# Transformer layer in fp32 pairs: the passage between the output projection and FFN2, and two orderings in the late FFN1 groups

## The reference

```
m_lat = silu(c) @ ada_w + ada_b          # nine shift/scale/gate vectors, also for c_ctx
x   = x   + 0.5 * m_lat[2] * swiglu(modulate(rms_norm(x, g1),   m_lat[0], m_lat[1]), W1in, W1out)
ctx = ctx + 0.5 * m_ctx[2] * swiglu(modulate(rms_norm(ctx, g1), m_ctx[0], m_ctx[1]), W1in, W1out)
mix = concat(retention(hx, hc), latent_attention(hx, hc)) @ mix_w_out
x   = x + m_lat[5] * mix
x   = x + 0.5 * m_lat[8] * swiglu(modulate(rms_norm(x, g3), m_lat[6], m_lat[7]), W2in, W2out)
out = rms_norm(x, final_g)
```

## Time and profile before

| | |
|---|---|
| profiled execution, its own time | 2855.02 us |
| its span | 2853.2 us |
| median of three runs | 2856.29 us |
| PE busy | 2775.5 us (97%), 12983 matmul records |
| PE weight load busy | 2293.5 us (80%) |
| DVE busy | 1699.8 us (60%) |
| ACT busy | 901.1 us (32%) |
| mean granted PE clock | 0.993 |
| chain that ended last | PE 83%, DVE 4%, ACT 3%, issue 2%, DMA 2% |

### The profile page before, as it was taken

The page is one execution under the profiler, slowest core; times in us unless marked ns, Lnnn a source line. Parts: engine busy times, 40 slices in busy tenths (PEclk is TensorE's granted clock), DMA queues, the critical chain, the costliest instruction groups (busy, mean ns, idle before and its releaser), DMA issues.

```text
span 2853.2 us, 33123 instructions
## 1 busy us (share of the span) xinstructions
PE 2775.5 (97%) x12983; PEld 2293.5 (80%) x12983; DVE 1699.8 (60%) x1740; ACT 901.1 (32%) x830; POOL 7.0 (0%) x15
## 2 busy tenths in 40 slices
PE   6999999999999999999999899999989999999998
PEld 4778888888888888878877788887878888888886
DVE  6866756666575756565645843465564555555556
ACT  6631212122121212112112522354353333333333
POOL 0000000000000000000000000000000000000000
PEclk9999999999999999999999999999999999999999
DMA  9956555555554657676755442432355555555553
GB/s 312 303 193 191 170 150 158 163 160 162 147 176 132 196 158 255 191 245 188 232 170 176 111 118 89 131 106 80 118 171 173 187 186 190 191 191 190 182 188 132
DMA packets 408016, 496.83 MB, mean 174 GB/s; under 512 B 19090, under 2 KB 277512, under 8 KB 407176
## 3 DMA queue, kind: packets, MB, share of 16 engines
q1 hardware_dynamic: 407196, 493.10, 55.3%
q0 software_dynamic: 496, 2.63, 0.3%
q10 hardware_dynamic: 252, 0.10, 0.0%
HBM read 493.69 MB, written 2.10 MB: 174 GB/s over the span
## 4 chain that ended last, share of the span: by engine, by line
PE 83%; DVE 4%; ACT 3%; issue 2%; DMA 2%; SPq 0%; DVEq 0%; ACTq 0%
PE py L944 8%; PE py L946 8%; PE py L945 8%; PE pg L944 5%; PE pg L946 5%; PE pg L945 5%; PE pu L946 5%; PE pu L945 5%; PE pu L944 5%; ACT wh L562 2%; PE py L1378 2%; PE py L1380 2%; PE py L1379 2%; PE pg L1359 1%; PE pg L1360 1%
## 5 line engine op out<-in xcount | busy, mean ns | idle before, releaser
L1450 DVE TENSOR_TENSOR wl<-raw,wh 128x2048 fp32r<-128x2048 f32 x342 | 783.7, 2291 | 832.5 <-ACT wh L562 832.3
L562 ACT ACTIVATE wh<-raw 128x2048 fp32r<-128x2048 f32 x342 | 654.1, 1914 | 1361.8 <-PE py L946 495.8
L944 PE MATMUL py<-ah,wh 128*128 128x512 f32 x704 | 276.8, 393 | 6.2 <-DVE xy L1612 5.1
L946 PE MATMUL py<-ah,wl 128*128 128x512 f32 x704 | 274.8, 390 | 0.0
L945 PE MATMUL py<-al,wh 128*128 128x512 f32 x704 | 274.6, 390 | 0.0
L944 PE MATMUL pu<-hh,wh 128*128 128x512 f32 x656 | 255.8, 390 | 0.0
L944 PE MATMUL pg<-hh,wh 128*128 128x512 f32 x656 | 255.5, 389 | 0.0
L946 PE MATMUL pu<-hh,wl 128*128 128x512 f32 x656 | 255.2, 389 | 0.0
L946 PE MATMUL pg<-hh,wl 128*128 128x512 f32 x656 | 255.2, 389 | 0.0
L945 PE MATMUL pu<-hl,wh 128*128 128x512 f32 x656 | 255.2, 389 | 0.0
L945 PE MATMUL pg<-hl,wh 128*128 128x512 f32 x656 | 255.2, 389 | 0.0
(11 more groups left out here) (420 smaller groups left out, 4605.2 us busy)
## 6 DMA issues: line engine op xcount, KB each, us to landing
raw<-in_ffn_w_in SPq DMA_DIRECT2D x170, 1024.0 KB
chunk<-in_ada_w SPq DMA_DIRECT2D x189, 512.0 KB, 3.9
raw<-in_ffn_w_out SPq DMA_DIRECT2D x88, 1024.0 KB
raw<-in_ada_w SPq DMA_DIRECT2D x64, 512.0 KB
raw<-in_mix_w_in SPq DMA_DIRECT2D x30, 1024.0 KB
accc<-in_ada_w SPq DMA_DIRECT2D x35, 512.0 KB, 4.7
raw<-in_mix_w_out SPq DMA_DIRECT2D x16, 1024.0 KB
war<-in_ffn_w_in SPq DMA_DIRECT2D x16, 384.0 KB, 5.1
```

Source lines behind the costliest of these rows:

```text
L562: nc.scalar.activation(wh[:, slot % 2, :], raw[:, slot, :], ACT.Copy).then_inc(wh_ready, 1)
L944: mm(out_ap, w[0], xh_ap, start=first, stop=False, skip_group_check=True)
L946: return mm(out_ap, w[1], xh_ap, start=False, stop=last, skip_group_check=True)
L1450: tt(wl[:, slot % 2, :], raw[:, slot, :], wh[:, slot % 2, :].bitcast(F32), ALU.subtract).then_inc(wl_ready, 1)
```

## The change

Three parts, and no arithmetic is changed.

**Passage.** The natural turns get a new order (`NATURAL`): the four of the gate first, then the eight of x. Turns 0 to 2 stand ahead of `square_sums(1)`, turns 3 to 5 behind it, and the remaining six behind half slabs 3, 4 and 5. `diag` moves to another place in memory (where low tiles 8 to 15 will be written) and DVE makes it ahead of the last output slabs. ACT loads the root's table ahead of the last squares, copies turns 0 and 1 ahead of the root, turns 2 to 5 behind tile 3, and the rest behind the tiles. DVE forms the low half of FFN2's second slab behind tile 3 in place of ahead of tile 0.

**Late loop.** In steps 8 and later no chunk piece goes ahead of the evictions.

**Last group.** SP issues the two input pieces ahead of the two chunk loads.

```diff
-    diag = at("diag", [P, KT, P], F32, o_e)
+    diag = at("diag", [P, KT, P], F32, o_hl + 8 * KB)
+    NATURAL = (8, 9, 10, 11, 0, 1, 2, 3, 4, 5, 6, 7)
 SP:
             for s in range(GSLABS - RAW):
                 ahead(LASTG, s)
+                x_piece(2 * s)
+                x_piece(2 * s + 1)
                 for t in (2 * s, 2 * s + 1):
                     chunk_load(8 * D + CH, t, t % 2, CHUNK0 + 3 * SINGLE_CHUNKS + t)
-                x_piece(2 * s)
-                x_piece(2 * s + 1)
 ACT:
             for s in range(8):
                 if s < 7:
                     static_split(MIX0 + S_OUTM + s + 2)
+                else:
+                    link(nc.scalar.activation(dummy[:], dummy[:], ACT.Sqrt))
                 for t in (2 * s, 2 * s + 1):
                     square(1, t, Y_OUT + HEADS + s + 1)
+            natural(0)
+            natural(1)
             roots(1)
             static_split(FFN2_0 + 1)
             for t in range(KT):
                 hh_tile(1, 0, ml[:, 6 * KT:7 * KT], t)
+                if t == 3:
+                    for p in range(2, 6):
+                        natural(p)
             for j in range(3, 8):
-                natural(2 * j - 6)
-                natural(2 * j - 5)
+                if j < 6:
+                    natural(2 * j)
+                    natural(2 * j + 1)
 PE:
+            natural_turn(0)
+            natural_turn(1)
+            natural_turn(2)
             square_sums(1)
+            for p in range(3, 6):
+                natural_turn(p)
             for j in range(8):
                 half_slab(0, FFN2_0 + j, ...)
-                if j >= 2:
-                    natural_turn(2 * j - 4)
-                    natural_turn(2 * j - 3)
+                if 2 < j < 6:
+                    natural_turn(2 * j)
+                    natural_turn(2 * j + 1)
 DVE:
-                    if units == 2 and todo:
+                    if units == 2 and todo and s < 2 * GROUP:
                         chunk_ops(*todo[0])
                         todo = todo[1:]
             static_split(MIX0 + S_OUTM + 1)
+            for t in range(KT):
+                ins = ts(diag[:, t, :], eyes[:, 0, :], g3l[:, t:t + 1], None, ALU.mult)
+            ins.then_inc(diag_ready, 1)
             roots(1, 0)
-            static_split(FFN2_0 + 1)
             for t in range(KT):
                 hl_tile(1, 0, xl, a3l, ml[:, 6 * KT:7 * KT], t)
+                if t == 3:
+                    static_split(FFN2_0 + 1)
+                    ve.wait_ge(nat_turned, 4)
-            for t in range(KT):
-                ins = ts(diag[:, t, :], eyes[:, 0, :], g3l[:, t:t + 1], None, ALU.mult)
-            ins.then_inc(diag_ready, 1)
```

More of the change, by code:

```diff
@@ L859, in _, with natural @@
             static_split(MIX0 + S_OUTM + 1)
+            def natural(p):
+                j = NATURAL[p]
+                se.wait_ge(nat_turned, p + 1)
+                dst = xn[:, j // 4, (j % 4) * 512:(j % 4 + 1) * 512] if j < 8 else g3b[:, (j - 8) * 512:(j - 7) * 512]
+                nc.scalar.activation(dst, py[p % 4][:], ACT.Copy).then_inc(y_free, 1)
             for s in range(8):
@@ L873, in _ @@
             link(nc.scalar.activation(dummy[:], dummy[:], ACT.Silu))
[L875 to L878, removed]
             def silu(i, m):
@@ L905, in _ @@
                 static_split(FFN2_0 + j + 2)
-            natural(10)
-            natural(11)
             with se.Fori(0, GROUPS - 2) as i:
@@ L1347, in _, with natural_turn @@
                     out_slab(MIX0 + S_OUTM + s, py[s], HEADS)
+            def natural_turn(p):
+                j = NATURAL[p]
+                pe.wait_ge(y_free, Y_F2 + p - 3)
+                if p == 0:
+                    pe.wait_ge(diag_ready, 1)
+                for t in range(4):
+                    o = py[p % 4][:, t * P:(t + 1) * P]
+                    if j < 8:
+                        ins = nc.tensor.transpose(o, xl[:, 4 * (j % 4) + t, (j // 4) * P:(j // 4 + 1) * P], ident)
+                    else:
+                        ins = mm(o, ones[:], diag[:, 4 * (j - 8) + t, :], start=True, stop=True)
+                ins.then_inc(nat_turned, 1)
+            natural_turn(0)
+            natural_turn(1)
+            natural_turn(2)
             square_sums(1)
+            for p in range(3, 6):
+                natural_turn(p)
             def half_slab(i, m, banks, quarter, first_tile=None):
@@ L1384, in down_slab @@
                         ins.then_inc(y_done, 1)
[L1386 to L1396, removed]
             pe.wait_ge(y_free, Y_F2)
```

## The result

| | before | after |
|---|---|---|
| median of the runs | 2855.81 us (4 runs, 2853.49 to 2858.62) | 2834.97 us (4 runs, 2833.67 to 2836.46) |
| profiled execution | 2855.02 us | 2833.67 us |
| its span | 2853.2 us | 2831.9 us |
| mean granted PE clock | 0.993 | 0.994 |

The ratio is 0.9924, with a 95% interval of 0.9912 to 0.9936: faster by 20.8 us. Between the two profiled executions it is 21.35 us.

A forecast was written before the change was run, and what follows sets the result against it. PE was taken as the bound (83% of the last-ending chain), with waits at three places: 6.7 + 8.8 + 5.7 = 21.2 us off 2855.02 gives 2833.8, plus 1.27 to the runs' median: 2835.1 us, range 2830 to 2842.

The forecast's parts named there:

- Last group, 8.8: Last group: PE's waits for x and ctx over seven slabs vanish once input pieces go first; 8.8 us gained.
- The ring rival: Last group: late chunk loads close SP's queue on itself, 18 us a slab, about 2879 us in all; chance 0.03.
- The 6.6 us of slack: Last group: chunk loads are used 6.6 us after the last lands; the ring forms only if they land later than that.
- Passage, 2.14 + 3.56 = 5.7: Passage: half slab 4 starts 2.14 us earlier, two gate pairs leaving PE's later stretch save 3.56; loop 5.7 us earlier.
- The wait ahead of half slab 3: Passage: DVE and ACT set the pace up to tile 15, so PE waits some 1.4 us there.
- the tiles' start: Passage: with the split gone from their front, DVE's tiles begin 2.1 us earlier.
- The rival "bound further on": Passage: slabs 5 to 7 also wait for ACT and DVE, only 2.14 us is left, 2838.7 us; chance 0.12.
- what the prediction left at 0 to 0.5: Passage: cost if the clock stays low behind the gap and the first half slab ends a microsecond later; 0 to 0.5.
- Late loop, 5.9 + 1.7 - 0.9 = 6.7: Late loop: eviction stalls gone 5.9 us, low clock behind one stall 1.7, less 0.9 new lateness at step 10; 6.7 gained.
- Its 0.3 a group: Late loop: the fourth load's piece comes 0.1 to 0.2 us late for step 10's turns, with the semaphore 0.3 a group.
- One of the prediction's signs of being wrong: Anywhere in the kernel: low clock in new places, listed among the observations that would show the prediction wrong; no size given.
- The rival that the prediction drew from it: Late loop: each stall could cost 0 or 1.7 us in another execution, returning 0 to 5.1, not 1.7; no chance given.

The follow-up runs named there:

- e5: The kernel before with one step alone: DVE forms the low half of FFN2's second slab behind tile 3, not ahead of tile 0; 2852.55 us.
- e4: The changed kernel with one step taken back: DVE forms the low half of FFN2's second slab ahead of tile 0 again; 2837.72 us.
- e3: The kernel before with only the passage's edits, late loop and last group as before; 2849.84 us.
- e2: The kernel before with only the input pieces issued ahead of the chunk loads in the last group; 2847.34 us.
- e7: The changed kernel with the first chunk piece of step 8 put between the evictions and the split; 2834.50 us.
- e1: The kernel before with only the late loop's edit, no chunk piece ahead of the evictions in step 8; 2849.97 us.
- e9: The changed kernel again, unedited, timed beside other kernels; 2835.71 us.
- f2: The changed kernel again, unedited, timed in another set on another chip; 2834.22 us.
- e6: The changed kernel with the passage's later splits behind tiles 6, 9, 12, ACT's copies behind the splits and Silu's table load later; 2835.22 us.

## Why the prediction was right

The time (2835.1 forecast, 2834.97 measured) came out by its own steps in two places. In the third the steps were right and the size belonged to one execution, so that the closeness of the total is in part luck.

**Last group, 8.8.** Measured 8.70, and 8.68 alone. The argument was one of order: the pieces' load is issued when its buffer is free and not behind two loads that wait for DVE. It also lands sooner than I took (median 3.6, not 4.8). The two chunk loads no longer stand just ahead of it; that this is the reason isn't shown. The ring rival asked that chunk loads land late; in the trace they are issued 3.6 us later than the pieces and hold nobody. The 6.6 us of slack in it was read too large: in before's trace the second of the two loads lands at 1464.85 and its operation starts at 1470.43, 5.6 us later. In the changed kernel these are 1457.36 and 1463.75, 6.4 us.

**Passage, 2.14 + 3.56 = 5.7.** Measured 2.36 + 3.53 = 5.89. e5 and e4 give each term by itself (2.44 and 3.60). The wait ahead of half slab 3 was 1.15 where I had 1.4. The square sums came 0.1 late, as worked out (2077.32 - 2074.53 = 2.79 against 2.68). The missing 0.2 is the tiles' start: 2.3 us earlier and not 2.1. What the prediction doesn't say is that some 1.1 of this term (the estimate above) is time that the low clock had cost the kernel before. The rival "bound further on" fell: no wait ahead of half slabs 5 to 7. e3 answers what the prediction left at 0 to 0.5, a low clock in the changed kernel: 0.

**Late loop, 5.9 + 1.7 - 0.9 = 6.7.** Measured 6.3 between the two profiled executions, in the mean 4.8. The table's rows take it apart. Late loop less stalls is 362.01 - 5.09 = 356.92 in before and 361.02 - 4.09 = 356.93 in e2; both had a stretch of low clock. It is 358.21 - 2.91 = 355.30 in e3 and 358.61 - 3.30 = 355.31 in e5, which had none. So one such event costs 1.62 (I had 1.7). With neither stall nor wait it is 354.41 (three executions), so a stall costs 0.89 / 3 = 0.30 beside its idle time (I had 0.26; e7's order differs too, so this is an estimate). Beyond these 354.41 the changed loop takes 0.3 to 1.3, mean 0.8, which I put down to the new wait (I had 0.9). Its 0.3 a group doesn't follow from its own numbers: 1141.2 + 3.9 + 1.28 is 1146.38, 0.03 and not 0.1 to 0.2 behind 1146.35. The load took 4.0 (1140.86 to 1144.86), and PE waited 0.29. On average each price came out within 0.1 us. What was mis-sized is the count: idle 5.1 where four executions have 5.1, 4.1, 2.9 and 3.3, and one clock event where four have two. The mean is 3.85 + 0.9 + 0.8 - 0.8 = 4.8. The prediction said this of the clock and not of the stalls. Their length hangs on when a 512 KB load lands: in all twelve DVE's first piece waited for its load, and PE's idle time is that wait less 0.22 (2.11 and 1.89 in the earlier trace rows).

Why did the time still come out? By the traces' means the change is worth 19.4, and 21.2 was forecast. Before's profiled late loop was 2.0 over its mean, but that execution was short elsewhere: 0.4 below the mean of thirteen executions up to group 7's first turns (1091.04 against 1091.44), 0.6 below it from slab 8 to the projection's end (545.64 against 546.27). So its total was an ordinary one (0.8 below the median of the runs shown above), which takes up about half of the 2.0. The rest is luck as far as the runs show: the medians say 20.4 to 20.8 and the three stretches 19.4, and those 1.0 to 1.4 us are not explained.

One of the prediction's signs of being wrong did show, low clock in a new place: the changed kernel's profile has 6.8 us of it from 50.2 us on, where before's has none. It lies ahead of all that was changed, and e1, e4, e9 and f2 have it there too (3.4 to 6.8 us) and the other seven not, e2 and e3 among them.

The Trainium skill ("TensorE: Matmul & The Clock Gate", "What's actually happening") has the clock judged in a rhythm that is independent of the kernel. The runs are in line with that: of twelve eviction stalls two were followed by low clock, group 8's 2.25 us in before and group 7's 1.91 in e2, while group 7's 1.89 in before was not. The rival that the prediction drew from it, a clock term that changes from one execution to the next, is what the four old loops show: 1.6 us in two and none in two.

## What to carry to other kernels

Ask of each operation in an engine's queue not what it costs but who stands behind it: all the gains here came from order and none from less work, the largest from issuing a load that can go ahead of two that can't. When stalls end on a DMA, price them from several executions, for one profile is one draw (here 5.1 us where the mean is 3.9). And where a faster PE runs into a chain of two other engines, look for what sets that chain's start: moving the split gave 2.4 us at once (e5), and moving the later ones another 2.3 (e6).

## What the runs showed that I had not expected

Thirteen profiled executions show what the clock does behind the gap of the passage. PE stands 2.4 us, does the square sums, and stands 4.0 to 6.3 us more in the four kernels without turns there (before, e1, e2, e5). All four then show the lower level, in before for some 10 us (window 2092 to 2104, same columns as the earlier trace rows):

```profile
2092.00:2104.00 12.00, 5.10 (x14) 3.74 (x15) 10.04 (x17) 6.62 (x10) 2.23 (x2) 0.57 0.59 213
```

With turns in the gap six of nine executions kept the upper level throughout, though PE still stood 2.26 us (the changed kernel; its half slab 0 begins at 2081.99):

```profile
2080.00:2086.00 6.00, 4.01 (x15) 2.60 (x16) 5.68 (x11) 4.38 (x10) 0.00 (x0) 1.00 0.37 153
```

Three of nine (e3, f2, and e4 with its 4.54 us) fell for some 3 us (below, 6 x 0.28 / 0.5 = 3.4). f2_after is the same program as the one above:

```profile
2080.00:2086.00 6.00, 4.16 (x12) 3.33 (x13) 5.68 (x11) 4.38 (x10) 0.00 (x0) 0.72 0.37 153
```

So with work in the gap the fall was rarer and shorter, and not excluded. Whether the turns do that, or the shorter idle time behind them (2.26 us against 4.0 to 6.3), isn't shown: the one kernel with turns and a long wait, e4, fell, in its one profiled execution. What a fall costs depends on who waits for PE. In the changed order nothing does (e3, f2). In e4 it cost up to 0.8 us, in the kernel before some 1.1, in the late loop 1.6, and in the mixer 2.8, in a place that no edit touches.
